# A decoder layer on one core: two banks for the spatial products, normalisation on ScalarE, three weight splits on VectorE

## The reference, cut to what matters

```python
x = x + 0.5 * swiglu(rms_norm(x, g_ffn1), w1_ffn1, w3_ffn1, w2_ffn1)
z = rms_norm(x, g_mix) @ w_in + b_in
q, k, v, u, vg = jnp.split(z, SPLITS, axis=-1)
attn_out, k_state, v_state = attend(q, k, v)          # window of 128, softmax with a sink
vg = layer_norm(jax.nn.gelu(vg), gm_ln_g, gm_ln_b)    # over 512 columns of each position
gm_out = jax.nn.gelu(u) * chunk_spatial_mix(vg.reshape(B, S, GM_GROUPS, GM_DIM), gm_w_s, gm_b_s)
x = x + jnp.concatenate([attn_out, gm_out], axis=-1) @ w_out + b_out
x = x + 0.5 * swiglu(rms_norm(x, g_ffn2), w1_ffn2, w3_ffn2, w2_ffn2)
gate = jax.nn.sigmoid(rms_norm(x, g_ple) @ w_ple_gate)
x = x + gate * (ple @ w_ple_proj)
# chunk_spatial_mix: in each chunk of 128 positions and each of 4 groups of 128 columns, tril(W_s[g]) @ v + b_s[g]
```

## Time and profile before

| what | us |
|---|---|
| median of three runs | 996.93 |
| the profiled execution's own time | 998.08 |
| span of the profiled execution | 996.3 |
| PE busy | 971.6 (98%) |
| DVE busy | 673.2 (68%) |
| ACT busy | 456.6 (46%) |
| POOL busy | 278.3 (28%) |

### The profile page before, as it was taken

One profiled execution on the slowest core, in us unless ns is written; L12 is line 12 of the kernel. 1 busy time (PEld: TensorE's weight loads), 2 busy tenths in 40 slices (PEclk: granted clock), 3 DMA queues, 4 the chain that ended last, 5 costly groups with the idle time before them and its releaser, 6 DMA issues.

```text
span 996.3 us, 19264 instructions
## 1 busy us (share of the span) xinstructions
PE 971.6 (98%) x7965; PEld 956.7 (96%) x7965; DVE 673.2 (68%) x999; ACT 456.6 (46%) x742; POOL 278.3 (28%) x155
## 2 busy tenths in 40 slices
PE   6999999999999999999999999999999999999996
PEld 5999999999999999999989999999999999999995
DVE  5799657856768563456875399757756758755575
ACT  6644424532544444555434455434543444445132
POOL 2303202211111226321448412301311111215461
PEclk9999999999999999999999999999999999999998
DMA  7952433252243327221114693243324224234202
GB/s 213 165 122 73 129 96 104 67 159 66 63 128 106 96 75 206 76 64 43 44 54 128 127 170 96 75 127 96 96 87 126 85 64 138 79 111 140 73 14 86
DMA packets 192178, 101.38 MB, mean 102 GB/s; under 512 B 13018, under 2 KB 189492, under 8 KB 192076
## 3 DMA queue, kind: packets, MB, share of 16 engines
q1 hardware_dynamic: 176624, 90.76, 32.1%
q0 software_dynamic: 11440, 5.77, 4.7%
q10 hardware_dynamic: 4028, 3.63, 1.2%
HBM read 97.59 MB, written 3.59 MB: 102 GB/s over the span
## 4 chain that ended last, share of the span: by engine, by line
PE 89%; DVE 5%; DMA 2%; ACT 2%; POOL 1%; issue 1%; SPq 0%; DVEq 0%; ACTq 0%
PE ps L1612 52%; PE ps L1692 32%; DMA w_raw<-in_w_ffn_dram 1%; PE ps L1648 1%; POOL h_lo L1061 1%; PE ps L1929 1%; DMA x_rows<-in_x_prompt_dram 1%; PE ps L1902 1%; DVE ab L1325 0%; ACT w_hi L693 0%; ACT h_hi L800 0%; PE ps L1643 0%; DVE mix_lo L1499 0%; DVE rs_t L1143 0%; DVE xb_lo L1177 0%
## 5 line engine op out<-in xcount | busy, mean ns | idle before, releaser
L1692 PE MATMUL ps<-xo_lo,w_hi 128*128 128x260 f32 x1008 | 284.7, 282 | 0.0
L1692 PE MATMUL ps<-xo_hi,w_lo 128*128 128x260 f32 x1008 | 284.4, 282 | 0.0
L1692 PE MATMUL ps<-xo_hi,w_hi 128*128 128x260 f32 x1008 | 284.2, 282 | 0.0
L1612 PE MATMUL ps<-h_hi,w_hi 128*128 128x260 f32 x960 | 195.8, 285 | 2.0 <-POOL h_lo L1061 1.2
L1612 PE MATMUL ps<-h_lo,w_hi 128*128 128x260 f32 x960 | 193.6, 283 | 0.0
L1612 PE MATMUL ps<-h_hi,w_lo 128*128 128x260 f32 x960 | 193.6, 283 | 0.0
L1692 PEld LDWEIGHTS ps<-xo_hi,w_lo 128*128 128x128 f32 x1008 | 189.8, 188 | 0.0
L1692 PEld LDWEIGHTS ps<-xo_lo,w_hi 128*128 128x128 f32 x1008 | 189.7, 188 | 0.0
L1692 PEld LDWEIGHTS ps<-xo_hi,w_hi 128*128 128x128 f32 x1008 | 189.6, 188 | 0.0
L1054 POOL TENSOR_TENSOR w_lo<-w_a,w_hi 128x512 fp32r<-128x512 f32 x36 | 66.8, 1857 | 307.6 <-ACT w_hi L762 307.6
L1612 PEld LDWEIGHTS ps<-h_hi,w_hi 128*128 128x128 f32 x960 | 148.2, 189 | 3.6 <-issue 3.4
(11 more groups left out here) (253 smaller groups left out, 1436.5 us busy)
## 6 DMA issues: line engine op xcount, KB each, us to landing
w_raw<-in_w_ffn_dram SPq DMA_DIRECT2D x88, 256.0 KB, 3.0
w_a<-in_w_ffn_dram SPq DMA_DIRECT2D x36, 512.0 KB, 4.9
w_raw<-in_w_ffn_dram SPq DMA_DIRECT2D x48, 384.0 KB, 3.5
w_raw<-in_w_ffn_dram SPq DMA_DIRECT2D x16, 512.0 KB, 6.1
w_lo<-in_w_ffn_dram POOLq DMA_DIRECT2D x11, 512.0 KB, 9.4
w_raw<-in_w_in_dram SPq DMA_DIRECT2D x10, 512.0 KB, 4.0
w_raw<-in_w_ple_gate_dram SPq DMA_DIRECT2D x8, 512.0 KB, 3.9
x_rows<-in_x_prompt_dram SPq DMA_DIRECT2D x4, 512.0 KB, 5.5
```

The lines of the kernel that those rows point to most:

```text
L1612: ins = pe.matmul(ps[:, bank + step * h, 0:HALF], w[:, c, w0:w0 + P], m_[:, sk, h * HALF:(h + 1) * HALF], start=(first and n == 0), stop=( ...
L1692: ins = pe.matmul(ps[:, b, 0:Q], w[:, c, k * P:(k + 1) * P], m_[:, op, k, :], start=(first and k == 0 and n == 0), stop=(k == 3 and n == 2 ...
```

## The change

Three things are changed.

1. The spatial products of groups 0 and 2 stay in bank 4, those of 1 and 3 go to bank 6. Group g now waits for DVE to have taken group g-2, and group 1 for the last probabilities to have been copied out of bank 6. The sample products of all four groups are done ahead of group 0, in 8 columns each, and DVE copies the 32 columns once to `s_sp`.
2. The normalisation of the rows moves from DVE to ACT, as `v * rs + (-mean * rs)`. DVE makes the bias in two small operations behind `norm_rsqrt`. It keeps its place (12, 1) in the list of steps.
3. The low halves of output weight tiles 0, 1 and 2 are made on DVE, at (13, 2), (13, 6) and k step 6 of output tile 0, and no longer on POOL.

In the diff the first `kind == "norm"` is in ACT's list, `split_lo` in POOL's, the list of three places and all up to the copy to `s_sp` in DVE's, the last piece in PE's.

```diff
+        first_out = [("out", m) for m in range(3)]
+        by_pool = {key: i for i, key in enumerate(key for key in index if key[0] != "down" and key not in summed
+                                                  and key not in first_out)}
...
+            elif key in first_out:
+                eng.wait_ge(out_lo, first_out.index(key) + 1)
...
+                elif kind == "norm":
+                    b = arg[0]
+                    n = P if b < NB else TS
+                    v = g_rows[0:n, b, :]
+                    act.wait_ge(norm_ready, 2)
+                    nc.scalar.activation(v, v, ACT.Identity, bias=mv[0:n, b, 0:1],
+                                         scale=rs[0:n, b:b + 1]).then_inc(g_centred, 1)
...
-                if key[0] == "down":
+                if key[0] == "down" or key in first_out:
...
+                if [kind, *arg] in (["gemm", 13, 2], ["gemm", 13, 6], ["out", 0, 6]):
+                    key = first_out[{2: 0, 6: 1}[arg[1]] if kind == "gemm" else 2]
+                    dve.wait_ge(w_hi_ready, index[key] + 1)
+                    nc.vector.tensor_tensor(w_at(wl, key), w_at(w_raw, key), w_at(wh, key).bitcast(F32),
+                                            ALU.subtract).then_inc(out_lo, 1)
...
                 elif kind == "norm_rsqrt":
                     rsqrt()
-                elif kind == "norm":
-                    nc.vector.tensor_scalar(v, v, mv[0:n, b, 0:1], rs[0:n, b:b + 1], ALU.subtract,
-                                            ALU.mult).then_inc(g_centred, 1)
+                    nc.vector.scalar_tensor_tensor(out=mv[:, 0:NB, 0:1], in0=mv[:, 0:NB, 0:1], scalar=-1.0,
+                                                   in1=rs[:, 0:NB].unsqueeze(2), op0=ALU.mult,
+                                                   op1=ALU.mult).then_inc(norm_ready, 1)
...
+                    if g == 0:
+                        link(nc.vector.tensor_copy(s_sp[:].rearrange("p g s -> p (g s)"), ps[:, 5, 384:384 + GG * TS]))
-                                                   in0=ps[:, 4, :].rearrange("p (b t) -> p b t", t=P),
+                                                   in0=ps[:, 4 + 2 * (g % 2), :].rearrange("p (b t) -> p b t", t=P),
...
-                    if g:
-                        pe.wait_ge(spatial_taken, g)
+                    if g > 1:
+                        pe.wait_ge(spatial_taken, g - 1)
+                    elif g:
+                        pe.wait_ge(probs_taken, 16)
```

More of the change, by code:

```diff
@@ L430, in hybrid_decoder_layer @@
             s_o = sb("s_o", [P, TS, NQ], scope=s)
+            s_sp = sb("s_sp", [P, GG, TS], scope=s)
         with ExitStack() as s:
@@ L469, in hybrid_decoder_layer @@
         gate_made, x_added = sem("gate_made"), sem("x_added")
-        w_negated, down_lo = sem("w_negated"), sem("down_lo")
+        w_negated, down_lo, out_lo = sem("w_negated"), sem("down_lo"), sem("out_lo")
         lo_in = [sem(f"lo_in{i}") for i in range(2)]
@@ L484, in hybrid_decoder_layer @@
         ws_summed, bs_ready = sem("ws_summed"), sem("bs_ready")
+        norm_ready = sem("norm_ready")
         g_centred, g_gained, g_normed = sem("g_centred"), sem("g_gained"), sem("g_normed")
@@ L555, in hybrid_decoder_layer @@
         summed = [("up", 0, n) for n in range(2, N_STD)] + [("up", 1, n) for n in range(3, N_STD)]
-        by_pool = {key: i for i, key in enumerate(key for key in index if key[0] != "down" and key not in summed)}
+        first_out = [("out", m) for m in range(3)]
+        by_pool = {key: i for i, key in enumerate(key for key in index if key[0] != "down" and key not in summed
+                                                  and key not in first_out)}
         def lo_wait(eng, key):
@@ L1376, in _ @@
             for kind, *arg in steps:
-                if kind == "stat_sum":
+                if [kind, *arg] in (["gemm", 13, 2], ["gemm", 13, 6], ["out", 0, 6]):
[3 more added lines that the diff above has]
+                                            ALU.subtract).then_inc(out_lo, 1)
+                elif kind == "stat_sum":
                     stat_diag(1)
@@ L1463, in _ @@
                     rsqrt()
-                elif kind == "norm":
-                    b = arg[0]
-                    n = P if b < NB else TS
-                    v = g_rows[0:n, b, :]
-                    nc.vector.tensor_scalar(v, v, mv[0:n, b, 0:1], rs[0:n, b:b + 1], ALU.subtract,
-                                            ALU.mult).then_inc(g_centred, 1)
+                    nc.vector.scalar_tensor_tensor(out=mv[:, 0:NB, 0:1], in0=mv[:, 0:NB, 0:1], scalar=-1.0,
+                                                   in1=rs[:, 0:NB].unsqueeze(2), op0=ALU.mult,
+                                                   op1=ALU.mult).then_inc(norm_ready, 1)
+                    nc.vector.scalar_tensor_tensor(out=mv[0:TS, NB, 0:1], in0=mv[0:TS, NB, 0:1], scalar=-1.0,
+                                                   in1=rs[0:TS, NB:NB + 1], op0=ALU.mult,
+                                                   op1=ALU.mult).then_inc(norm_ready, 1)
                 elif kind == "ws_sum":
@@ L1488, in _ @@
                                                    op0=ALU.mult, op1=ALU.add)
-                    nc.vector.tensor_scalar(sp[:, TP:T], ps[:, 5, 384:384 + TS], col(C_LNG + g), bs_all[:, g, 0:1],
+                    nc.vector.tensor_scalar(sp[:, TP:T], s_sp[:, g, :], col(C_LNG + g), bs_all[:, g, 0:1],
                                             ALU.mult, ALU.add).then_inc(spatial_taken, 1)
@@ L1943, in _ @@
                     pe.wait_ge(w00_ready, 1)
-                    if g:
-                        pe.wait_ge(spatial_taken, g)
+                    if g > 1:
+                        pe.wait_ge(spatial_taken, g - 1)
+                    elif g:
+                        pe.wait_ge(probs_taken, 16)
                     else:
                         pe.wait_ge(s_out, 1)
+                    if g == 0:
+                        for g_ in range(GG):
+                            pe.matmul(ps[:, 5, 384 + g_ * TS:384 + (g_ + 1) * TS], g_rows[0:TS, NB, g_ * P:(g_ + 1) * P],
+                                      w00_diag[:, g_, :], start=True, stop=True)
                     for b in range(NB):
-                        pe.matmul(ps[:, 4, b * P:(b + 1) * P], g_rows[:, b, g * P:(g + 1) * P], ws_t[:, g, :],
+                        ins = pe.matmul(ps[:, 4 + 2 * (g % 2), b * P:(b + 1) * P], g_rows[:, b, g * P:(g + 1) * P], ws_t[:, g, :],
                                   start=True, stop=True)
-                    pe.matmul(ps[:, 5, 384:384 + TS], g_rows[0:TS, NB, g * P:(g + 1) * P], w00_diag[:, g, :],
-                              start=True, stop=True).then_inc(spatial_made, 1)
+                    ins.then_inc(spatial_made, 1)
                 elif kind == "s_scores":
```

## The result

The changed kernel takes 1002.32 us (median of six runs, 1002.19 to 1002.87). The kernel before, run six times beside and ahead of it, has 998.68 (996.17 to 999.42; the three runs shown at first were the low end). The ratio is 1.0038, with a 95% interval of 1.0028 to 1.0049. It is slower, by 0.4%. The forecast was 997.3, within 994.0 to 999.9, with 0.16 for slower.

What follows compares the result with a forecast made beforehand. PE, busy 98% of the span, was taken as the bound. Old wait -3.89 plus new wait with its clock loss +4.23 gave +0.34 us; 996.93 + 0.34 = 997.3 us, range 994.0 to 999.9.

Steps and rivals of the forecast that it cites:

- The old wait: Mixer, PE's third spatial product (group 2) waiting for DVE: goes away, -3.89 us, 2.43 of waiting and 1.46 of clock.
- The new wait of `values`: Mixer, PE's `values` of item 7 wait for ACT's copy of the probabilities, behind the normalisations: +2.77 us.
- The row that I took for ACT: ACT's five normalisations, priced from an Identity 520 wide at 0.62 each: 3.10 us, bounds 2.85 to 3.60.
- POOL's split did catch the inverse root: Ahead of the normalisation, POOL's split of input tile 13 makes an operation of DVE's inverse root take 2.36 us.
- The clock behind the new wait: PE after the wait of `values`: lower granted clock costs 1.46 us, as behind the old wait; bounds 0 and 1.7.
- The sample products at 0: PE's eight short sample passes, done in a row ahead of group 0: cost 0, bounds -0.1 to +0.3 us.
- The splits on DVE at nothing: Output tiles' splits on DVE: 1.22 us each, 3.7 in all, behind work PE does meanwhile, so priced at nothing.
- The slower rival's second wait, at the last step of output tile 0: PE waits 1 us there for group 3's low half and may lose 1.46 of clock: 999.8 us; chance 0.14.
- The rival "clock stays up": The wait of `values` comes but the clock does not fall behind it: -1.12 us, 995.8; chance 0.18.
- The baseline: The kernel before, whole execution: median 996.93 us, to which the forecast added its +0.34.

Runs made afterwards that it cites:

- experiment 5: The repeat: the changed kernel once more, unchanged, in a later series; 1002.64 us, ratio 1.0041 to the kernel before.
- experiment 8: Changed kernel with ACT's normalisations behind the copy of item 7's probabilities and input tile 13's split on DVE; 994.63 us, ratio 0.9975 to before.
- experiment 1: Changed kernel with ACT's five normalisations behind, not ahead of, the copy of item 7's second half of probabilities; 995.57 us, ratio 0.9975 to before.
- experiment 9: experiment 1 with item 7's values, sample and spatial products later in PE's list, and PE waiting for all normalisations ahead of (12, 5); 1002.08 us.
- experiment 6: experiment 1 with PE made to wait for all five normalisations ahead of item 7's `values`; 1001.61 us, ratio 1.0030 to before.
- experiment 2: Changed kernel with the normalisation back on DVE in its old form; 995.79 us, ratio 0.9981 to before.
- experiment 10: experiment 9 without PE's wait for the normalisations, the later list kept; 998.42 us, ratio 0.9994 to before.
- experiment 3: Kernel before with only the two banks and the sample products in one go, normalisation on DVE, splits on POOL; 996.88 us, ratio 0.9981.
- experiment 11: experiment 8 with item 7's `values` at (12, 7), spatial 0 with sample products at (13, 0), spatial 1 at (13, 2); 995.62 us, ratio 0.9961 to before.
- experiment 12: experiment 8 with only the samples' values moved, from (12, 4) to (12, 2); 994.76 us, ratio 0.9953 to before.

## Why the prediction was wrong, point by point

- **The old wait goes**: right. Group 2's product waits for nothing in any version with two banks, and there is no low clock around it.
- **The new wait of `values`**: right in its place, its releaser and its size. The sum gave 2.77; it is 2.05 in the first profile and 2.82 in the second. The 2.05 are the 2.8 less what PE lost to the half clock ahead of the wait. That the size fits is in part luck. The five normalisations took 3.54 rather than 3.10, 0.44 more; from the root's end to ACT's start it took 0.28 instead of 0.40 (491.15 to 491.43), the copy 0.57 instead of 0.60, and the release of PE 0.05 instead of 0.15 (495.54 to 495.59), 0.25 less together. The row that I took for ACT, 0.62 from start to start, has an operation of another kind behind it; its length, 0.72, my upper bound, was the better guide. By the Trainium skill, "ScalarE: Activation LUTs", section "Rules for kernel authors", which budgets about 0.3 us and 0.83 ns an element, one of them takes 0.725, an estimate. The trace agrees, with 0.71 each. POOL's split did catch the inverse root, 2.38 us long beside 2.39, as the forecast had it.
- **The clock behind the new wait: the step that failed.** This term of the sum was mis-sized. I took 1.46 us, the price behind the old wait, with bounds 0 and 1.7, and chose it because the waits are alike in length. The clock was at 1.2 GHz for 13.6 us and in the repeat for 10.2, against 3.4. Free of idle time the changed kernel's stretch is 34.2 us (36.54 - 2.38); that of experiment 8, at full clock, is 28.6, and of experiment 1 29.1. So the term is 5.0 to 5.5 us, three times its upper bound; the repeat gives 4.5 to 5.0 (36.71 - 3.14 = 33.6). The length of the wait does not set it: behind idle times of 2.28, 2.34, 2.39 and 2.82 us (before, experiments 9, 6 and 5) the low clock cost 1.46, 2.4, 4.4 and 4.5. What differs is what stands behind. The old wait had a spatial product and then k steps behind it; this one has `values`, one k step, the sample products and a spatial product. That this sets the price is likely and rests on one profile each; why the clock stays down longer there stays open. Nor is "behind the wait" the whole of it: in the first profile the clock fell ahead of the wait, as it does without a long wait in experiments 2 and 10. What the wait does is make it fall in every execution: none of the 18 of the changed kernel and experiment 6 is under 1001.5, where 36 of the 48 of experiments 1, 2, 3 and 8 are under 998.
- **The sample products at 0**: wrong by some 1.1 us in the kernel's favour, outside the bounds of -0.1 and +0.3. Each group took 1.37 us on PE before, spatial and sample passes together (497.87 to 499.24, rows 2). Now group 0 takes 1.90 with all sample products (495.17 to 497.07 in experiment 1) and each of the other three 0.81 (510.23 to 511.04): 1.90 + 3 x 0.81 = 4.3 against 5.5. In a row the sample products cost 0.98 (495.17 to 496.15), 0.25 a group; between products of 128 columns each group's pair cost 0.56 (1.37 - 0.81). So the change of form and back cost 0.31 a group, more than the matmuls of 8 columns themselves.
- **The splits on DVE at nothing**: they cost nothing on the path, and are a gain of 1.4 us once the banks are there (experiments 2 and 3).
- **The slower rival's second wait, at the last step of output tile 0**: it exists, 0.33 us instead of 1. It was the wrong reason for slower.
- **The rival "clock stays up"** got 0.18, and its opposite, a clock that stays down longer, nothing. By the runs: -3.9 + 2.05 + 5.5 - 1.1 + 0.3 = +2.9, and the stretch measured +3.04.
- **The baseline**: the three runs of before had a median of 996.93; more of them give 998.7 to 999.7, since the kernel before has executions from 996 to 1004. So of the 5.0 us between 997.3 and 1002.3, 1.7 are the baseline's (998.68 for 996.93); 3.3 are the change's, +3.64 measured for +0.34 forecast.

## What to carry to other kernels

Price a stall of PE with what stands behind it: after idle times of 2.3 to 2.4 us the low clock cost 1.5 us in the kernel before, 2.4 in front of long matmuls and 4.4 in front of passes of 8 and 64 columns, in one profile each. Before work is added ahead of an instruction in an engine's list, look for the one copy there that PE waits for, and put the addition behind it. Try short passes on PE further apart, with long steps between them, and take ten executions or more where a kernel's times come in two groups.

## What was not expected of the hardware

- The granted clock fell with PE 1.00 busy in every window from 489 on, in experiment 2 (at 490.9, 13.6 us) and in the second kernel of 9 and 10 (at 491.5, 3.4 us), both times at the end of 16 matmuls of 8 columns that take 1.9 us. The Trainium skill, "TensorE: Matmul & The Clock Gate", section "A second HAM failure mode: psum-queue depth-cycling", tells of another kernel (bf16, 512 columns) whose clock goes up and down because PE stands still briefly and often between groups of matmuls. These profiles agree that no long wait is needed; whether there are such brief standstills in them, windows with PE 1.00 busy neither show nor exclude.
- A kernel's executions can fall into two groups 5 to 6 us apart with nothing between them (995.2 to 996.3 and 1000.5 to 1002.2, eight and four of twelve). The one profile from an upper group has the low clock in the mixer, those from lower groups have none there. The versions with the wait of 2.0 us or more have no lower group.
- What sets how often the clock falls without a wait was not measured beyond experiments 11 and 12.
